# Two neighbouring rows of each expert's weights per partition, and VectorE outputs written in the matching order

## The reference, cut to what matters

```
x = layer_norm(ALPHA * x + mix, ln1_g, ln1_b)              # 256 x 1024
logits = x @ router_w + router_b                           # 1024 x 32
# for each expert e, on the tokens that chose it:
gu   = xb @ w_gate_up[e] + b_gate_up[e]                    # 1024 x 2048
gate = min(gu[:, :1024], 7);  up = clip(gu[:, 1024:], -7, 7)
act  = gate * sigmoid(1.702 * gate) * (up + 1)
y    = act @ w_down[e] + b_down[e]                         # 1024 x 1024
x = layer_norm(ALPHA * x + ffn, ln2_g, ln2_b)
```

## Time and profile before

| | us |
|---|---|
| median of 3 runs | 1185.83 |
| lowest and highest of them | 1183.32, 1187.58 |
| the profiled execution, its own time | 1187.94 |
| its span in the trace | 1185.9 |
| TensorE busy | 1073.7 (91%) |
| VectorE busy | 265.7 (22%) |
| ScalarE busy | 145.9 (12%) |
| packets on the SP queue | 81914, 425.37 MB, 89.0% of 16 DMA engines |

### The profile page before, as it was taken

How to read it: one execution, slowest core, us unless ns; L and a number is a source line. 1 busy time by engine, 2 the same in 40 slices (tenths; PEclk the granted TensorE clock), 3 DMA queues, 4 the chain that set the end, 5 groups by cost and what they waited for, 6 DMA issues and landing times.

```text
span 1185.9 us, 14722 instructions
## 1 busy us (share of the span) xinstructions
PE 1073.7 (91%) x5364; PEld 456.6 (38%) x5365; DVE 265.7 (22%) x770; ACT 145.9 (12%) x313; POOL 29.2 (2%) x54
## 2 busy tenths in 40 slices
PE   7999898889999999888889879999999898989884
PEld 6777545333333333323232323333333233332321
DVE  2354653131211111111111201121211111111114
ACT  2043511010111000000000100000010000010100
POOL 3001300000000000000000000000000000000000
PEclk9999997999999999999999989999999999999998
DMA  9723439665999999999999998999999999999994
GB/s 310 254 97 72 182 152 381 266 256 207 416 418 418 418 418 419 418 418 418 418 418 418 418 417 352 417 418 417 418 417 419 418 418 417 418 417 418 417 411 163
DMA packets 82515, 426.32 MB, mean 359 GB/s; under 512 B 6057, under 2 KB 9690, under 8 KB 49690
## 3 DMA queue, kind: packets, MB, share of 16 engines
q1 hardware_dynamic: 81914, 425.37, 89.0%
q10 hardware_dynamic: 576, 0.61, 0.2%
HBM read 424.91 MB, written 1.05 MB: 359 GB/s over the span
## 4 chain that ended last, share of the span: by engine, by line
PE 54%; DMA 24%; SPq 16%; DVE 3%; issue 2%; ACT 1%; DVEq 0%
PE PB L755 52%; DMA WB<-in_w_gate_up_dram 19%; SPq L350 9%; SPq L345 5%; DMA WB<-in_w_down_dram 5%; DVE S L1509 0%; DMA X<-in_x_dram 0%; DVE K L1499 0%; ACT S L657 0%; PE PB L1109 0%; SPq L354 0%; DVE S L1482 0%; PE PB L762 0%; DVE WB L1401 0%; DVE S L1718 0%
## 5 line engine op out<-in xcount | busy, mean ns | idle before, releaser
L755 PE MATMUL PB<-WB,S 128*64 128x512 f32 (+5 forms) x3456 | 766.0, 594 | 66.8 <-DMA WB<-in_w_gate_up_dram 34.6
L755 PEld LDWEIGHTS PB<-WB,S 128*64 128x64 f32 (+2 forms) x3456 | 249.4, 139 | 562.2 <-issue 452.0
L1610 DVE TENSOR_SCALAR S<-PB 128x512 f32<-128x512 f32 (+1 forms) x34 | 23.5, 691 | 665.5 <-PE PB L755 665.5
L755 PE MATMUL PB<-S 32*64 32x512 f32 (+5 forms) x464 | 106.4, 585 | 4.3 <-ACT S L689 1.4
L693 ACT ACTIVATE S<-S 128x512 f32<-128x512 f32 x32 | 20.2, 630 | 554.2 <-DVE S L1610 554.2
L755 PEld LDWEIGHTS PB<-S,X 128*128 128x128 f32 x512 | 61.2, 200 | 13.3 <-issue 12.2
L755 PE MATMUL PB<-S,X 128*128 128x128 f32 x512 | 64.3, 286 | 1.0 <-DVE S L1553 1.0
L755 PE MATMUL PB<-S,WB 128*128 128x256 f32 (+2 forms) x336 | 61.7, 383 | 0.4 <-ACT S L531 0.4
L755 PEld LDWEIGHTS PB<-S 32*64 32x64 f32 (+5 forms) x464 | 34.3, 147 | 64.4 <-issue 54.0
L755 PEld LDWEIGHTS PB<-S,WB 128*128 128x128 f32 (+1 forms) x336 | 47.9, 174 | 12.0 <-issue 2.1
L1654 DVE COPY S<-PB 64x512 f32<-64x512 f32 x32 | 21.9, 683 | 132.4 <-PE PB L755 132.4
(11 more groups left out here) (208 smaller groups left out, 342.9 us busy)
## 6 DMA issues: line engine op xcount, KB each, us to landing
WB<-in_w_gate_up_dram SPq DMA_DIRECT2D x128, 2048.0 KB, 23.0
WB<-in_w_down_dram SPq DMA_DIRECT2D x128, 1024.0 KB, 22.7
WB<-in_w_in_dram SPq DMA_DIRECT2D x3, 2048.0 KB, 16.1
WB<-in_w_in_dram SPq DMA_DIRECT2D x1, 2144.0 KB, 11.3
WB<-in_w_in_dram SPq DMA_DIRECT2D x2, 1024.0 KB, 10.8
WB<-in_w_out_dram SPq DMA_DIRECT2D x2, 1024.0 KB, 10.3
WB<-in_w_out_dram SPq DMA_DIRECT2D x1, 2048.0 KB, 7.9
WB<-in_w_in_dram SPq DMA_DIRECT2D x1, 1040.0 KB, 12.6
```

Source lines behind the costliest of these rows:

```text
L755: return mm_(o, l, r, start=start, stop=stop, skip_group_check=True)
L1610: ts(g, gate, LIMIT, None, ALU.min).then_inc(s[g_ok], 1)
```

## The change

Three things change together; no instruction is added, removed or put in another place.

1. The rows of `w_gu` and `w_dn` are dealt to the partitions in another way: partition p gets rows 512h + 4p + m for h = 0, 1 and m = 0 to 3, and a quarter is two rows that lie next to each other in memory. A quarter is then 128 runs of 16 KB (gate and up) or 8 KB (down). The sizes, the number, the slots and the order of the DMAs are as before. The router weights are dealt in the same way, with runs of 512 B for 128 B.
2. The other operand of each product must have its rows in the same order, and it gets it where DVE writes it. The output of the first layer norm (L1514, when called for `x_sb`) and the clipped gate and up (L1610, L1611) are read in order and written with neighbouring elements 128 elements (512 B) apart, four at a time.
3. The sum before the second layer norm (L1718) reads `x_sb` with the same steps of 512 B and writes in order.

```diff
-            gu_v = w_gu[0].rearrange("e (k p) n -> e p k n", p=P)
-            dn_v = w_dn[0].rearrange("e (k p) n -> e p k n", p=P)
+            gu_v = w_gu[0].rearrange("e (h p m) n -> e p h m n", p=P, h=2)
+            dn_v = w_dn[0].rearrange("e (h p m) n -> e p h m n", p=P, h=2)
...
-                sp.dma_start(gu_slot[par][:, kk * c:kk * c + kk, :], src[:, kk * c:kk * c + kk, :]).then_inc(s_gul[par][c], 16)
+                sp.dma_start(gu_slot[par][:, kk * c:kk * c + kk, :], src[:, c // 2, 2 * (c % 2):2 * (c % 2) + 2, :]).then_inc(s_gul[par][c], 16)
...
-                sp.dma_start(dn_slot[:, kk * c:kk * c + kk, :], src[:, kk * c:kk * c + kk, :]).then_inc(s_dnl[par][c], 16)
+                sp.dma_start(dn_slot[:, kk * c:kk * c + kk, :], src[:, c // 2, 2 * (c % 2):2 * (c % 2) + 2, :]).then_inc(s_dnl[par][c], 16)
...
-            sp.dma_start(rw, router_w[0].rearrange("(k p) e -> p k e", p=P)).then_inc(s["ln_ld"], 16)
+            sp.dma_start(rw.rearrange("p (h m) e -> p h m e", h=2),
+                         router_w[0].rearrange("(h p m) e -> p h m e", p=P, h=2)).then_inc(s["ln_ld"], 16)
...
+            def by_rows(a):
+                return a.rearrange("p (m q) -> p q m", q=P)
+            def in_order(a):
+                return a.rearrange("p (q m) -> p q m", q=P)
...
-                    yield stt(dst[:, b, c], v[:, b, c], st[:, o + 2:o + 3], bt[:, c], ALU.mult, ALU.add)
+                    yield stt(place(dst[:, b, c]), view(v[:, b, c]), st[:, o + 2:o + 3], view(bt[:, c]), ALU.mult, ALU.add)
...
-                for ins in norm(y, b, b + 1, lng, lnb, x_sb, "ln_ld"):
+                for ins in norm(y, b, b + 1, lng, lnb, x_sb, "ln_ld", by_rows, in_order):
...
-                ts(g, gate, LIMIT, None, ALU.min).then_inc(s[g_ok], 1)
-                ts(u, up, LIMIT, -LIMIT, ALU.min, ALU.max).then_inc(s[clip], 1)
+                ts(by_rows(g), in_order(gate), LIMIT, None, ALU.min).then_inc(s[g_ok], 1)
+                ts(by_rows(u), in_order(up), LIMIT, -LIMIT, ALU.min, ALU.max).then_inc(s[clip], 1)
...
-                    ins = stt(yf[:, b, 512 * h:512 * h + 512], x_sb[:, b, 512 * h:512 * h + 512], ALPHA,
-                              PB[2 * b + h][:, :], ALU.mult, ALU.add)
+                    c = slice(512 * h, 512 * h + 512)
+                    ins = stt(in_order(yf[:, b, c]), by_rows(x_sb[:, b, c]), ALPHA, in_order(PB[2 * b + h][:, :]), ALU.mult,
+                              ALU.add)
```

More of the change, by code:

```diff
@@ L30 @@
 DN_CHUNKS = 4
+assert KT == 2 * GU_CHUNKS == 2 * DN_CHUNKS
 ALPHA = 2.0 ** 0.25
@@ L337, in _ @@
                         sp.dma_start(bV[:, at:at + n], b_in[0:1, c:c + n].broadcast_to([P, n])).then_inc(s["bv_ld"], 16)
-            gu_v = w_gu[0].rearrange("e (k p) n -> e p k n", p=P)
-            dn_v = w_dn[0].rearrange("e (k p) n -> e p k n", p=P)
+            gu_v = w_gu[0].rearrange("e (h p m) n -> e p h m n", p=P, h=2)
+            dn_v = w_dn[0].rearrange("e (h p m) n -> e p h m n", p=P, h=2)
             def load_gu(i, par, c):
                 kk = KT // GU_CHUNKS
-                src = gu_v[2 * i + par] if isinstance(i, int) else gu_v[bass.ds(2 * i + par, 1)].rearrange("e p k n -> (e p) k n")
-                sp.dma_start(gu_slot[par][:, kk * c:kk * c + kk, :], src[:, kk * c:kk * c + kk, :]).then_inc(s_gul[par][c], 16)
+                src = gu_v[2 * i + par] if isinstance(i, int) else gu_v[bass.ds(2 * i + par, 1)].rearrange("e p h m n -> (e p) h m n")
+                sp.dma_start(gu_slot[par][:, kk * c:kk * c + kk, :], src[:, c // 2, 2 * (c % 2):2 * (c % 2) + 2, :]).then_inc(s_gul[par][c], 16)
             def load_dn(i, par, c):
                 kk = KT // DN_CHUNKS
-                src = dn_v[2 * i + par] if isinstance(i, int) else dn_v[bass.ds(2 * i + par, 1)].rearrange("e p k n -> (e p) k n")
-                sp.dma_start(dn_slot[:, kk * c:kk * c + kk, :], src[:, kk * c:kk * c + kk, :]).then_inc(s_dnl[par][c], 16)
+                src = dn_v[2 * i + par] if isinstance(i, int) else dn_v[bass.ds(2 * i + par, 1)].rearrange("e p h m n -> (e p) h m n")
+                sp.dma_start(dn_slot[:, kk * c:kk * c + kk, :], src[:, c // 2, 2 * (c % 2):2 * (c % 2) + 2, :]).then_inc(s_dnl[par][c], 16)
             def count_extra_blocks(e):
@@ L1499, in half_stats, with norm @@
                 return dve.bn_stats(st[:, 12 * b + 6 * h:12 * b + 6 * h + 6], v[:, b, 512 * h:512 * h + 512])
-            def norm(v, b, n, g, bt, dst, loaded):
+            def by_rows(a):
+                return a.rearrange("p (m q) -> p q m", q=P)
+            def in_order(a):
+                return a.rearrange("p (q m) -> p q m", q=P)
+            def norm(v, b, n, g, bt, dst, loaded, place=lambda a: a, view=lambda a: a):
                 o = 24 + 4 * b
```

## The result

The changed kernel takes 1175.34 us (median of 7 runs, 1171.85 to 1179.91) against 1183.58 for the kernel before in the same comparison (7 runs, 1183.32 to 1187.58). The ratio is 0.991 with a 95% interval of 0.9891 to 0.9928, so the change saves 8.5 to 12.9 us. The forecast was 11.5 us less, 1174.3 us.

A forecast was written before the change was run, and what follows sets the result against it. The experts were taken as bound by DMA, 30.12 us each, over two streams of 28.3 experts. Saving 16.3 us there less 4.8 us for strided writes gave 11.5 us less, 1174.3 us from 1185.83, range 1162 to 1180.

The forecast's parts named there:

- The streams: Two gapless DMA stretches, 28.3 experts long: halved packets save 0.58 us an expert, 16.3 us (15.0 to 23.5).
- The fixed part: DMA engines' time for each packet whatever its size: taken as 9 ns, between 8.3 and 13.
- The page on DMA: Trainium skill's 3.5 ns a packet for the expert loads: saving would be 6.3 us, the program about 1184.
- The strided instructions, each: VectorE's strided instructions on 512 elements: each 0.39 us slower, between 0 and twice that.
- the term of 4.8 us: Exposed strided VectorE instructions before the first stream and at the end: 4.8 us lost (0 to 9.6).
- The 1.6 at the end: Final sum before the second layer norm: four strided reads on the chain cost 1.6 us.
- The 3.2 before the first stream: First layer norm 1.6 us, clips of expert 0 and first extra block 0.8 each: first stream starts later.
- The second extra block: Slower clips, 0.8 us, only eat TensorE's waits for down weights there; nothing is left at the end.
- The sum: Whole program: 16.3 us saved less 4.8 lost, 11.5 us less, 1174.3 us.
- Packets are not the unit: Rival: streams keep their rate, only VectorE's 4.8 us are left, 1190.6 us; chance 0.08.
- only down gains: Rival: runs above 8 KB are cut, gate and up keep their packets, 3.4 us saved, 1182.4 us; chance 0.10.
- longer runs suit memory less: Rival: partitions reading 32 KB apart cost 2% of the rate, 17 us, about 1208 us; chance 0.02.

The follow-up runs named there:

- e2: Changed kernel with the old loads of gate, up and down, keeping the strided VectorE instructions and the router's new load; 1190.19 us, ratio 1.0021 to the kernel before.
- e4: Kernel before with only down loaded by neighbouring rows (8 KB runs) and gt and ut written with steps; ratio 0.9931 to the kernel before.
- e6: Changed kernel with the two neighbouring rows of gate and up loaded by two DMAs of one row, 8 KB packets; 1182.33 us, ratio 0.9969 to the kernel before.
- e8: Changed kernel with down loaded in two DMAs of four neighbouring rows (16 KB runs); 1177.27 us, ratio 0.993 to the kernel before.
- e9: Changed kernel with gate and up loaded from the second turn on in two DMAs of four neighbouring rows (32 KB runs); 1178.44 us, ratio 0.9923 to the kernel before.
- e10: Changed kernel with both down and gate and up loaded by halves (16 KB and 32 KB runs); 1179.74 us, ratio 0.9938 to the kernel before.
- e12: The changed kernel itself, run again as a yardstick for e11; ratio 0.9903 to the kernel before.
- e1: Kernel before with only the new loads of gate, up and down, VectorE writes and router load as before; 1170.16 us, ratio 0.9858 to the kernel before.
- e3: Kernel before with only gate and up loaded by neighbouring rows (16 KB runs) and x_sb written and read with steps; ratio 0.9966 to the kernel before.
- e5: Kernel before with each quarter of gate and up loaded by two DMAs of half the columns (4 KB runs); 1203.75 us, ratio 1.0143 to the kernel before.
- e7: Changed kernel with steps moved from writes to reads in the clips and the norm's last instruction; 1174.60 us beside the coarser loads, ratio 0.9897 to the kernel before.
- e11: Changed kernel with down by halves except the last expert's by quarters, clips reading PSUM with steps and writing whole; ratio 0.9908 to the kernel before.

## Why the prediction was right

**The streams.** 28.3 experts times 0.58 us was 16.3 us; loads alone give 16.8, the profiled streams 15.2. The turn of 59.05 us was forecast as 59.1, the 426 GB/s as such. The fixed part was taken as 9 ns between 8.3 from the rates and 13 from the occupied time; over the whole series it is 9.4, or 8.9 with the completions counted. (The occupied times as printed give 13.8 and not 13, so the range should have begun near 1160.) The argument that decided between the two, that the first adds up to the measured 30.12 us and the second overlaps, held: 13 ns would have made the turn 58.6.

**The page on DMA.** By the 3.5 ns of the Trainium skill ("DMA: Bandwidth & Descriptors", Why small descriptors are slow) the turn would have been 59.8 us, as an estimate; it is 59.05. The measurement decides for the rows.

**The strided instructions, each.** Forecast 0.39 us, measured 0.34 to 0.38. Row L1300, with steps of 144 B, was a good neighbour for steps of 512 B. The Trainium skill's "Vector Engine (DVE) Microarchitecture Reference" (5.2) agrees at the lower end of the estimate made from it, 0.34 us, and not at the 0.74 of steps of 24 words.

**The strided instructions, on the path.** Here the term of 4.8 us was too large: alone they cost 0.7 to 4.1. The 1.6 at the end were 1.4. The 3.2 before the first stream were forecast to start it 3 us later, and in the profile it starts 0.4 later. They are there as durations, and the chain of the changed kernel carries them:

```profile
212.46 1.05 DVE S L1621
213.51 0.89 DVE S L1622
...
223.65 25.77 PE PB L758 x136
249.44 0.61 ACT S L660
```

The end of DVE's last instruction there is 215.84 us for 214.15 before, 1.7 late (0.55 of it already ahead of the first strided instruction, at 172.87 for 172.32); yet ScalarE's L660 starts at 249.44 where L657 started at 249.36. The stretches between show what gave it back. Before:

```profile
221.87 27.47 PE PB L755 x136
```
```profile
215.00:222.00 7.00, 3.63 (x11) 1.38 (x11) 1.88 (x10) 0.87 (x2) 0.00 (x0) 1.00 1.01 414
222.00:236.00 14.00, 14.00 (x58) 4.64 (x59) 0.00 (x0) 0.00 (x0) 0.00 (x0) 0.88 0.32 131
```

After:

```profile
215.00:222.00 7.00, 6.01 (x14) 2.66 (x14) 2.67 (x12) 0.60 (x2) 0.00 (x0) 0.76 1.04 434
222.00:236.00 14.00, 12.35 (x58) 4.37 (x60) 0.00 (x0) 0.38 (x1) 0.00 (x0) 1.00 0.26 111
```

TensorE ran at its lower clock, 1.2 GHz, for a time in both; a mean of 0.88 or 0.76 is a mixture of that and 2.4. Before, that time fell on the dense matmuls of the second expert; after, on the few matmuls ahead of them, where there are idle gaps to take it up. By single microseconds it stands at 0.50 from 223 us on in the kernel before, behind a gap of TensorE of 3.37 us (up to 221.87), and from 217 on in the changed one, behind the wait for the clips, which has grown from 1.67 to 2.30 us. The 136 matmuls took 27.47 us and take 25.77, which is the 1.7.

The pattern goes with the clips in all fourteen profiles. In the second stretch the granted clock is 1.00 in the eight kernels' profiles with slow clips (`after`, `e2`, `e4`, `e6`, `e8`, `e9`, `e10`, `e12`) and 0.88 to 0.92 in the six with fast ones (`before`, `e1`, `e3`, `e5`, `e7`, `e11`). Why the clock falls where it does was not tried. The start of the first stream itself shows no cost of the strided instructions: 290.81 us in `e2`, which has them all, 290.95 in `e1`, which has none, and 289.66 to 293.64 over all but `e10` (295.95).

**The second extra block** was forecast to end no later, since TensorE waited for down there and the 0.8 us would eat those waits. In the changed kernel they eat more than the waits, and the chain runs through the clips:

```profile
680.78 1.02 DVE S L1621
681.83 1.05 DVE S L1622
...
686.18 6.06 PE PB L758 x32
```

It takes faster loads and slow clips together. With one of the two, in `e2` and in `e1`, the chain still goes through the landing of down; `e1`:

```profile
661.60 27.27 DMA WB<-in_w_down_dram
...
688.91 1.98 PE PB L755 x8
```

So it does in `e7`, which is the changed kernel with fast clips (landing at 690.32 us). From its first issue to its second it takes 418.74 us (292.43 to 711.17) and the changed kernel 419.34. So the slow clips cost about 0.6 us there where the prediction had nothing, within the streams' 15.2.

**The sum.** Against the forecast of 11.5 the pair of profiles has 13.4: 1.1 less from the streams, 2.8 less lost before them, 0.2 less at the end. The timed runs have 10.7 (8.5 to 12.9), and `e12` 11.5. The mechanism in the streams was right and is measured by itself. That the total meets the forecast to 1 us is in part luck: the term of 4.8 was too large, and how much TensorE's clock gives or takes in one execution, some 2 us at a place, was not in the sum at all.

**The rivals.** "Packets are not the unit" is refuted by `e5` (a dose of the other sign) and by the equal savings of `e3` and `e4`; "only down gains" by `e3` and by the 16 KB packets; "longer runs suit memory less" by `e6`.

## What to carry to other kernels

Where DMA engines are occupied throughout and a turn of the loop is bytes over a rate, count the packets: here each costs about 9 ns of an engine besides its bytes, from 4 to 32 KB, and dealing neighbouring rows to a partition halves them without moving more data. The permutation has to be paid somewhere; look for the side on which it is free (reads out of PSUM were) or covered. A coarser transfer that saves packets inside a stream can lose as much at the stream's ends, where work waits for a whole transfer (1.7 us at each start here); price both.

## What the runs showed that was not expected

- VectorE's clips read PSUM with steps of 16 B in the time of whole reads (692 ns for 691), while the norm's instruction with the same step out of SBUF takes 0.38 us more on 512 elements (1131 ns for 748), and a write into SBUF with steps of 512 B takes 0.36 to 0.38 more.
- Slower VectorE instructions before the first stream were given back by TensorE's clock, whose low time fell on sparse work in place of dense work (0.88 to 1.00 in the dense stretch); the repeated profile of the changed kernel shows the same clocks (0.76 and 1.00) and its first issue at 292.83 us for 292.59. The same 112 matmuls behind the second extra block took 23.91 us in most profiles and 25.64 to 25.87 in `e1`, `e2` and `e11`, at 0.91 to 0.93. A delay of 1 to 2 us in front of a dense stretch could not be priced from durations alone.
